# Sums over later keys from blocks added up first, and taken one unit later

## The reference

```
z         = q @ k.T * scale                        # per head, 512 x 512
log_beta  = log_sigmoid(z)
log_1mb   = where(key < query, log_beta - z, 0)
suffix    = reverse cumsum of log_1mb over keys, without the key itself
attn      = where(key < query, exp(log_beta + suffix), 0)
out       = attn @ v
```

## Time and profile before

| | us |
|---|---|
| median of 3 runs | 1727.99 (1726.3 to 1729.07) |
| the profiled execution, its own time | 1727.9 |
| its span in the trace | 1726.0 |
| PE busy | 1655.1 (96%) |
| DVE busy | 1036.1 (60%) |
| ACT busy | 798.5 (46%) |
| POOL busy | 710.0 (41%) |

### The profile page before, as it was taken

How to read it: one execution, slowest core, us unless ns; L and a number is a source line. 1 busy time by engine, 2 the same in 40 slices (tenths; PEclk the granted TensorE clock), 3 DMA queues, 4 the chain that set the end, 5 groups by cost and what they waited for, 6 DMA issues and landing times.

```text
span 1726.0 us, 19471 instructions
## 1 busy us (share of the span) xinstructions
PE 1655.1 (96%) x7340; PEld 1343.7 (78%) x7340; DVE 1036.1 (60%) x1173; ACT 798.5 (46%) x1001; POOL 710.0 (41%) x325
## 2 busy tenths in 40 slices
PE   3999999999989999999999999999899999999997
PEld 2778787877778888888887888777788787887875
DVE  6777788777637918816633767566337564255642
ACT  2665565666444425423342333666554443244442
POOL 1233343433355444444464443444364252442523
PEclk7999999999989999999999999999999999999999
DMA  9333333332233332332322231211133131331312
GB/s 363 134 111 123 122 116 117 96 124 86 73 104 98 96 99 86 101 131 90 97 83 90 88 104 60 70 54 55 38 98 98 37 110 40 109 96 42 105 49 73
DMA packets 46460, 166.87 MB, mean 97 GB/s; under 512 B 5152, under 2 KB 5280, under 8 KB 45856
## 3 DMA queue, kind: packets, MB, share of 16 engines
q1 hardware_dynamic: 46368, 165.63, 29.4%
HBM read 163.52 MB, written 2.10 MB: 96 GB/s over the span
## 4 chain that ended last, share of the span: by engine, by line
PE 84%; DVE 11%; ACT 2%; issue 1%; DMA 1%; POOL 1%; SPq 0%; DVEq 0%; ACTq 0%
PE lin L625 15%; PE lin L627 15%; PE lin L626 15%; PE big L625 7%; PE big L627 7%; PE big L626 7%; DVE scr L1538 1%; DVE cq_lo L1640 1%; DVE tmp L1667 1%; DVE tmp L2130 1%; PE big L742 1%; DVE tmp L1686 1%; PE big L744 1%; PE big L1033 1%; PE big L1032 1%
## 5 line engine op out<-in xcount | busy, mean ns | idle before, releaser
L599 POOL TENSOR_TENSOR w_lo<-raw,w_hi 128x1024 fp32r<-128x1024 f32 (+1 forms) x215 | 530.7, 2472 | 730.5 <-ACT w_hi L1069 730.3
L625 PE MATMUL lin<-h_hi,w_hi 128*128 128x512 f32 x952 | 375.5, 394 | 6.9 <-POOL w_lo L599 3.9
L627 PE MATMUL lin<-h_hi,w_lo 128*128 128x512 f32 x952 | 371.5, 390 | 0.0
L626 PE MATMUL lin<-h_lo,w_hi 128*128 128x512 f32 x952 | 371.2, 390 | 0.0
L1069 ACT ACTIVATE w_hi<-raw 128x1024 fp32r<-128x1024 f32 (+1 forms) x215 | 223.9, 1041 | 161.0 <-PE m_b L643 49.2
L625 PEld LDWEIGHTS lin<-h_hi,w_hi 128*128 128x128 f32 x952 | 179.1, 188 | 46.4 <-POOL w_lo L599 6.5
L627 PEld LDWEIGHTS lin<-h_hi,w_lo 128*128 128x128 f32 x952 | 179.0, 188 | 38.0
L626 PEld LDWEIGHTS lin<-h_lo,w_hi 128*128 128x128 f32 x952 | 179.2, 188 | 37.0 <-issue 0.7
L599 POOL TENSOR_TENSOR qk_hl<-raw,qk_hl 128x1024 fp32r<-128x1024 f32 (+1 forms) x44 | 109.4, 2490 | 164.7 <-ACT qk_hl L1069 164.7
L625 PE MATMUL lin<-y_hi,w_hi 128*128 128x512 f32 x324 | 127.3, 393 | 5.6 <-DVE y_lo L2135 3.0
L627 PE MATMUL lin<-y_hi,w_lo 128*128 128x512 f32 x324 | 126.1, 389 | 0.0
(11 more groups left out here) (455 smaller groups left out, 3217.1 us busy)
## 6 DMA issues: line engine op xcount, KB each, us to landing
raw<-weights SPq DMA_DIRECT2D x245, 512.0 KB, 3.6
slab<-ada SPq DMA_DIRECT2D x32, 512.0 KB, 4.5
scr<-ada SPq DMA_DIRECT2D x16, 512.0 KB, 6.3
raw<-weights SPq DMA_DIRECT2D x10, 256.0 KB, 2.8
x<-x_t SPq DMA_DIRECT2D x2, 1024.0 KB, 6.1
out_t<-scr SPq DMA_DIRECT2D x8, 256.0 KB, 2.0
raw<-weights SPq DMA_DIRECT2D x4, 448.0 KB, 3.4
rgw<-rg_w SPq DMA_DIRECT2D x1, 1024.0 KB, 7.3
```

The costliest lines, as they stand in the source:

```text
L599: nc.gpsimd.tensor_tensor(lo[:, 0:w], raw[:, s, 0:w], hi[:, 0:w].bitcast(F32), ALU.subtract).then_inc(w_split, 1)
L625: nc.tensor.matmul(psum_of(n), wh, hi(k), start=(k == 0), stop=False)
L626: nc.tensor.matmul(psum_of(n), wh, lo(k), start=False, stop=False)
L627: last = nc.tensor.matmul(psum_of(n), wl, hi(k), start=False, stop=(k == nk - 1))
```

## The change

`suffixes` takes 14 products in place of 20: 4 pairs with the strict matrix on the diagonal, and 3 pairs with the matrix of ones on sums of blocks. Those sums come from a new function `blocks_behind` on DVE: two additions in place in `att_b`, then for two of the three sums a copy of the high part and a subtraction for the low part; it raises `behind_done`. The third sum is the last diagonal block itself. In the loop, PE runs `suffixes(g)` after the units xr and yr and after `head_square(2h+2)`, where it ran before `head_square(2h+2)` and yr. On DVE, `blocks_behind` comes behind `square_low(2h+2)`, and the addition of line 1729 with its wait for `suffix_done` moves behind `convolve`, the k norm and the `accumulate` that follows. ACT, POOL and SP have the same lists as before.

```diff
+        behind_hi = [y_hi[:, 7, 0:3 * P], cq_hi[...][:, 1280 + T:2048], lm_hi[:, 896:1024]]
+        behind_lo = [y_lo[:, 7, 0:3 * P], cq_lo[...][:, 1280 + T:2048], lm_lo[:, 896:1024]]
...
-            def suffixes():
-                for j in range(TB):
-                    for i in range(j, TB):
-                        o = COL[j] + (i - j) * P
-                        sel = sel_r[:, 0 if i == j else 1]
-                        nc.tensor.matmul(big_f[:, o:o + KW[i]], sel, lm_hi[:, COL[i]:COL[i] + KW[i]], ...)
-                        last = nc.tensor.matmul(big_f[:, o:o + KW[i]], sel, lm_lo[:, COL[i]:COL[i] + KW[i]], ...)
+            def suffixes(g):
+                pe.wait_ge(lm_done, g + 1)
+                for j in (3, 0, 1, 2):
+                    out = big_f[:, COL[j]:COL[j] + KW[j]]
+                    cols = slice(COL[j], COL[j] + KW[j])
+                    nc.tensor.matmul(out, sel_r[:, 0], lm_hi[:, cols], start=True, stop=False)
+                    last = nc.tensor.matmul(out, sel_r[:, 0], lm_lo[:, cols], start=False, stop=(j == TB - 1))
+                pe.wait_ge(behind_done, g + 1)
+                for j in (2, 1, 0):
+                    out = big_f[:, COL[j] + P:COL[j] + KW[j]]
+                    nc.tensor.matmul(out, sel_r[:, 1], behind_hi[j], start=False, stop=False)
+                    last = nc.tensor.matmul(out, sel_r[:, 1], behind_lo[j], start=False, stop=True)
                 last.then_inc(suffix_done, 1)
...
-                    pe.wait_ge(lm_done, g + 1)
-                    suffixes()
                 if h == 0:
                     head_square(2, m_b[:])
                 elif h < HEADS:
                     pe.wait_ge(rooted, 2 * h + 1)
+                    if g >= 0:
+                        unit("yr", g, H, L)
                     head_square(2 * h + 2)
                 if g >= 0:
-                    unit("yr", g, H, L)
+                    suffixes(g)
...
+            def blocks_behind():
+                v.tensor_tensor(att_b[:, 1152:1280], att_b[:, 1152:1280], att_b[:, 896:1024], AD)...
+                v.tensor_tensor(att_b[:, 640:896], att_b[:, 640:896], att_b[:, 1024:1280], AD)...
+                for j, rows in ((1, att_b[:, 1024:1280]), (0, att_b[:, 512:896])):
+                    v.tensor_copy(behind_hi[j], rows)...
+                    v.tensor_tensor(behind_lo[j], rows, behind_hi[j].bitcast(F32), SU)...
...
                 square_low(2 * h + 2)
+                if g >= 0:
+                    blocks_behind()
                 if h < HEADS:
                     accumulate(ADA_FIRST + 4 * h)
...
                 if g >= 0:
                     convolve(g)
-                    dve.wait_ge(suffix_done, g + 1)
-                    v.tensor_tensor(att_a, att_a, z, AD).then_inc(att_t, 1)
                 if h < HEADS:
                     (k norm, accumulate)
                 if g >= 0:
+                    dve.wait_ge(suffix_done, g + 1)
+                    v.tensor_tensor(att_a, att_a, z, AD).then_inc(att_t, 1)
                     dve.wait_ge(att_exp, g + 1)
                     mask_products()
```

More of the change, by code:

```diff
@@ L268, in build @@
         lm_done = sem("lm_done")
+        behind_done = sem("behind_done")
         suffix_done = sem("suffix_done")
@@ L489, in build @@
         lm_lo = cq_lo[:].rearrange("p a t -> p (a t)")[:, 0:1280]
+        behind_hi = [y_hi[:, 7, 0:3 * P], cq_hi[:].rearrange("p a t -> p (a t)")[:, 1280 + T:2048], lm_hi[:, 896:1024]]
+        behind_lo = [y_lo[:, 7, 0:3 * P], cq_lo[:].rearrange("p a t -> p (a t)")[:, 1280 + T:2048], lm_lo[:, 896:1024]]
         sq_hi = [y_hi[:, 6], cq_hi[:].rearrange("p a t -> p (a t)")[:, 1280:1280 + T]]
@@ L828, in _ @@
             nc.tensor.matmul(m_a[:], rgw[:, 8 + g], A(S1["xr"], g), start=True, stop=True).then_inc(gates_done, 1)
-            pe.wait_ge(lm_done, HEADS)
-            suffixes()
+            suffixes(g)
             for m in range(3):
@@ L1641, in shifted_logs @@
                 dve.wait_ge(lm_done, counted(lm_done))
+            def blocks_behind():
+                v.tensor_tensor(att_b[:, 1152:1280], att_b[:, 1152:1280], att_b[:, 896:1024], AD).then_inc(dve_order, 1)
+                dve.wait_ge(dve_order, counted(dve_order))
+                v.tensor_tensor(att_b[:, 640:896], att_b[:, 640:896], att_b[:, 1024:1280], AD).then_inc(dve_order, 1)
+                dve.wait_ge(dve_order, counted(dve_order))
+                for j, rows in ((1, att_b[:, 1024:1280]), (0, att_b[:, 512:896])):
+                    v.tensor_copy(behind_hi[j], rows).then_inc(dve_order, 1)
+                    dve.wait_ge(dve_order, counted(dve_order))
+                    signal = dve_order if j else behind_done
+                    v.tensor_tensor(behind_lo[j], rows, behind_hi[j].bitcast(F32), SU).then_inc(signal, 1)
+                    dve.wait_ge(signal, counted(signal))
             def convolve(g):
@@ L1727, in _ @@
                     convolve(g)
-                    dve.wait_ge(suffix_done, g + 1)
-                    v.tensor_tensor(att_a, att_a, z, AD).then_inc(att_t, 1)
-                    dve.wait_ge(att_t, counted(att_t))
                 if h < HEADS:
@@ L1740, in _ @@
                 if g >= 0:
+                    dve.wait_ge(suffix_done, g + 1)
+                    v.tensor_tensor(att_a, att_a, z, AD).then_inc(att_t, 1)
+                    dve.wait_ge(att_t, counted(att_t))
                     dve.wait_ge(att_exp, g + 1)
```

## The result

| | us |
|---|---|
| before, median | 1728.42 (1726.3 to 1729.07, 4 runs) |
| changed, median | 1754.25 (1754.02 to 1754.73, 4 runs) |
| ratio | 1.0152, 95% interval 1.0134 to 1.0170 |
| changed, profiled execution: own time, span | 1754.3, 1752.5 |

The account below looks back on a forecast made before the run. The loop is nearly all PE's own work, but the change delays gb's weight past its slack: 1727.9 + 17.8 (late gb) - 0.6 (head 7) + 6.8 (clock falls) gives 1752 us, range 1742 to 1764.

Parts of the forecast that it names:

- `blocks_behind`: On DVE behind `square_low`: four additions or subtractions, two copies and gaps take 2.56 us per head, delaying everything behind.
- The moved addition: On DVE, line 1729 behind the k norm and an `accumulate`: 2.11 us later; its wait for `suffix_done` is free.
- From the addition's end to gb: Exponential and copy on ACT, then POOL's low part: gb's weight is ready 5.02 us after the addition's end.
- The sum without the clock: Late gb in the loop: 2.94 us in each of 4 odd passes, 2.00 in each of 3 even ones, +17.8 us.
- The clock: TensorE's clock falls to half behind PE's new waits before gb: 4 falls in 7 passes at 1.7 us, 6.8 us.
- PE's saving is worth nothing: In the loop, 0.57 us fewer products per head and 1.27 us less wait in odd passes only lengthen PE's wait.
- gb's bank: Freed at `gelu_done`, some 2 us behind ACT's copy while POOL needs 2.5: at about the same time, nothing lost.
- Head 7: No split hangs behind its exponential and `blocks_behind` lies in DVE's idle time: 0.57 us less, taken as -0.6.
- not slower: Rival: gb's weight isn't last, PE saves 4.6 us of products and 5.3 of waits: 1718 us; chance 0.06.
- the clock stays up: Rival: same late gb in the loop, but no fall of TensorE's clock: 1745 us; chance 0.20.
- a fall in every pass: Rival: same late gb, and TensorE's clock falls in all 7 passes: 1757 to 1760 us; chance 0.15.
- a split meet `blocks_behind`: Rival: a split of POOL stops DVE's `blocks_behind` in each pass, 15 us more: 1767 us; chance 0.02.

Follow-up runs that it names:

- Experiment 2: Changed kernel, ACT's split of gb's weight and gelu of yr ahead of the exponential: 1728.5 us, ratio 1.0003; same edit in kernel before: 1730.4 us, ratio 1.0000.
- the filled kernel: Changed kernel with products nobody reads filling PE's waits ahead of ga (odd passes) and gb: 1748.6 us, ratio 1.0117 to the kernel before.
- experiment 6: Changed kernel with unread products in PE's idle time, 7 ahead of ga in odd passes, 11 or 10 ahead of gb: 1748.6 us, ratio 1.0117.
- experiment 8: Changed kernel, split and gelu early on ACT, DVE order q norm, convolve, both accumulates: 14 products 1737.4 us (1.0056); 20 products without `blocks_behind` 1721.3 us (0.9959).
- experiment 7: Changed kernel, gb's split and gelu of yr ahead of ACT's exponential, and DVE's `convolve` directly behind `blocks_behind`: 1722.4 us, ratio 0.9967 to the kernel before.
- experiment 1: Changed kernel with only the split of gb's weight moved ahead of ACT's wait for `att_t` and exponential: 1755.0 us, ratio 1.0157 to the kernel before.
- experiment 5: Kernel before with the moves alone: 20 products behind yr, DVE's addition behind the k norm, no `blocks_behind`: 1736.8 us, ratio 1.0049.

## Why the prediction was right

- *The bound.* Right: the reading that counted was not PE's share but what stands behind line 1729. gb's weight had 1.73 and 2.67 us of slack, and the change asked for 4.67. Experiment 2 shows it from the other side: with gb's weight and bank freed from the exponential the loss is gone.
- *`blocks_behind`*, priced at 2.56 us from nearby shapes: 199.70 + 0.56 - 197.73 = 2.53 us. *The moved addition*, 2.11 us: 208.19 - 206.08 = 2.11.
- *Small slips.* 24 x 0.23 is 5.5, not 5.4. The two durations of the earlier trace rows are those of line 1636, in `shifted_logs`, and not of `mask_products`; line 1659, which is `mask_products`, shows nearly the same (0.291 and 2.378 us). Neither enters the sum.
- *From the addition's end to gb*, 5.02 us: 214.66 - 209.68 = 4.98. PE's waits, 4.8 and 2.6 us: 1.83 + 2.76 = 4.6 in pass 3, of which the first part before ga as said, and 2.47 in pass 2.
- *The sum without the clock*, +17.8 in seven passes: the filled kernel has 15.9 in six, and its first gate product is 3.3 us later than before (114.60 for 111.33); 0.2 of that stood already at the start of pass 1. Together 19: right within about a microsecond.
- *The clock*, 4 falls of 1.7 us, 6.8 together: in the profiled execution five, of which four (passes 3 to 6) were on the path and cost 6.1 us; the one in pass 1 cost nothing (experiment 6). That the number was right is luck: it was an interpolation, and which wait brings a fall I could not have said. Passes 2 and 7 waited 2.47 and 2.76 us before gb without a fall.
- *PE's saving is worth nothing*: right for the changed kernel. By experiment 8 it is worse than nothing in that order, where 14 products are 16 us slower than 20. Where PE doesn't wait for the late gb, it does show: experiment 7 is 0.3% faster than the kernel before, though a new order alone, with 20 products, gave as much (experiment 8).
- *Incomplete*: gb's bank. I wrote that it comes free "at about the same time" and counted one chain; there are two behind the exponential, and freeing the weight alone gains nothing, because PE then waits for the bank and DVE's addition comes later (experiment 1). Also unseen was the wait for the root of k in even passes, hidden by `blocks_behind` itself (experiment 5). Neither changed the sum.
- *Head 7*, -0.6 us: from pass 7's first gate product to the first product behind the wait for `y_lo` near 1250 us (below) are 836.05 us, for 836.68 before: -0.6, as said. From there to the span's end are 479.42 us, for 478.03: 1.4 us more, because the clock fell once behind that wait, far behind the change. This was no part of the forecast, and accounts for part of what the profiled execution took beyond it.

The rivals: "not slower" is refuted; "the clock stays up" is the filled kernel, 1748.6 for 1745; a fall in every pass did not happen. Nor did a split meet `blocks_behind`: its four additions and subtractions took 0.29, 0.43, 0.43 and 0.56 us in all eight heads, each within 4 ns.

## What to carry to other kernels

Before moving a wait later on one engine, list what stands behind the instruction that the wait releases, on the next engine too: here a weight's split and a bank's release stood behind an exponential only because the program had them in that order, and with the weight freed the bank alone still stopped TensorE. The cure was to issue them ahead of the exponential, not to save products. Moving the split also had a price on a third engine, which the same timelines show. And before moving work from the busiest engine to another, look at the other in the loop itself: DVE, 60% busy over the program, was busy 253 of the 330 us from 100 to 430, and in experiment 8 PE waited for it.

## What was not expected of the hardware

- The same wait with and without a fall of the clock. PE waits 2.36 us for line 1993's `y_lo` in the kernel before and goes on at full clock (first row). In the changed kernel the same wait, late in the program and untouched by the change, is followed by products at 1.2 GHz:

```profile
1248.00:1252.00 4.00, 3.75 (x15) 2.82 (x16) 2.01 (x3) 2.11 (x3) 0.00 (x0) 1.00 0.02 4
```
```profile
1273.08 0.80 PE L628 MATMUL lin<-y_hi,w_hi 128*128 128x512 f32 x1 [2.36 <-DVE y_lo L2014]
1273.68 0.63 PE L629 MATMUL lin<-y_lo,w_hi 128*128 128x512 f32 x1
```

  The length of the first product doesn't tell: it was 0.50 us in pass 2, without a fall, and in passes 4 to 6, with one. Of the six waits of 2.47 to 2.78 us before gb in the changed kernel four were followed by a fall, and each of these cost about 1.5 us. Executions of one kernel spread with it: the 20 of the kernel before on one chip lie between 1725.7 and 1731.4 us, those near 1726 with a mean clock of 0.989 or 0.990, those above 1730 with 0.986 or 0.987.
- DVE's accumulate, with two inputs in SBUF, took 1.28 us in the kernel before (1.285 to 1.287 in all 28 of line 1538 from 60 to 470 us). Beside a split of POOL it took up to 3.43 us (experiment 1), two of them 4.62 (experiment 8). In the kernel before none happened to meet one.
